# Second FFNs of a decoder trunk: three of four down pairs as seven half products

## The reference

```python
D_MODEL, SEQ, DEPTH, D_FF = 1024, 512, 2, 2816

def rms_norm(x, gain):
    xf = x * lax.rsqrt(jnp.mean(x * x, axis=-1, keepdims=True) + NORM_EPS)
    return xf * gain

def swiglu(x, w1, w3, w2):
    return (jax.nn.silu(x @ w1) * (x @ w3)) @ w2

for l in range(DEPTH):
    x = x + 0.5 * swiglu(rms_norm(x, ffn1_norm[l]), ffn1_w1[l], ffn1_w3[l], ffn1_w2[l])
    x = x + mixing(x)          # four branches, gates, W_out: not touched
    x = x + 0.5 * swiglu(rms_norm(x, ffn2_norm[l]), ffn2_w1[l], ffn2_w3[l], ffn2_w2[l])
```

## Time and profile before

| | us |
|---|---|
| median of 3 runs (lowest, highest) | 2750.36 (2749.57, 2750.45) |
| span of the profiled execution | 2748.1 |
| PE busy | 2743.3 |
| DVE busy | 1851.7 |
| ACT busy | 1335.1 |
| POOL busy | 940.7 |

### The profile page before, as it was taken

The page is one execution under the profiler, slowest core; times in us unless marked ns, Lnnn a source line. Parts: engine busy times, 40 slices in busy tenths (PEclk is TensorE's granted clock), DMA queues, the critical chain, the costliest instruction groups (busy, mean ns, idle before and its releaser), DMA issues.

```text
span 2748.1 us, 41845 instructions
## 1 busy us (share of the span) xinstructions
PE 2743.3 (100%) x16054; PEld 2337.2 (85%) x16054; DVE 1851.7 (67%) x2984; ACT 1335.1 (49%) x2103; POOL 940.7 (34%) x466
## 2 busy tenths in 40 slices
PE   9999999999999999999999999999999999999999
PEld 8898888777788889898998988887777888898988
DVE  7686857885667448585785878578846674585755
ACT  6353444655355346353563534446553653553533
POOL 0135824433343442131121357244333434421221
DMA  5333583222222232233332335832222222322332
GB/s 171 108 108 116 151 180 107 84 71 72 83 85 85 85 100 94 92 116 100 108 108 92 116 115 159 171 108 84 70 73 81 86 83 85 100 99 94 108 98 102
DMA packets 113110, 284.80 MB, mean 104 GB/s; under 512 B 35617, under 2 KB 45345, under 8 KB 112417
## 3 DMA queue, kind: packets, MB, share of 16 engines
q1 hardware_dynamic: 112928, 282.35, 34.6%
HBM read 268.67 MB, written 9.44 MB: 101 GB/s over the span
## 4 chain that ended last, share of the span: by engine, by line
PE 99%; DVE 1%; ACT 0%; issue 0%; DVEq 0%; ACTq 0%
PE bank L627 22%; PE bank L629 22%; PE bank L628 22%; PE bank L676 7%; PE bank L677 7%; PE bank L678 7%; PE bank L653 1%; PE bank L655 1%; PE bank L654 1%; PE bank L1048 1%; PE bank L1067 1%; PE bank L1082 1%; PE bank L817 1%; PE bank L1181 1%; PE bank L1035 0%; PE bank L1240 0%
## 5 line engine op out<-in xcount | busy, mean ns | idle before, releaser
L476 POOL TENSOR_TENSOR w_lo<-raw,w_hi 128x1024 fp32r<-128x1024 f32 x208 | 519.8, 2504 | 872.1 <-ACT w_hi L468 872.1
L627 PE MATMUL bank<-h_hi,w_hi 128*128 128x512 f32 x1504 | 593.4, 395 | 0.5 <-DVE silu_a L2363 0.3
L629 PE MATMUL bank<-h_hi,w_lo 128*128 128x512 f32 x1504 | 585.8, 390 | 0.0
L628 PE MATMUL bank<-h_lo,w_hi 128*128 128x512 f32 x1504 | 585.8, 390 | 0.0
L468 ACT ACTIVATE w_hi<-raw 128x1024 fp32r<-128x1024 f32 x310 | 326.5, 1056 | 353.8 <-PE bank L629 313.5
L541 POOL TENSOR_TENSOR w_lo<-raw,w_hi 128x1024 fp32r<-128x1024 f32 x122 | 223.4, 1854 | 802.3 <-DVE bank L2308 802.3
L627 PEld LDWEIGHTS bank<-h_hi,w_hi 128*128 128x128 f32 x1504 | 282.3, 188 | 65.6 <-issue 7.1
L629 PEld LDWEIGHTS bank<-h_hi,w_lo 128*128 128x128 f32 x1504 | 282.4, 188 | 59.8
L628 PEld LDWEIGHTS bank<-h_lo,w_hi 128*128 128x128 f32 x1504 | 282.5, 188 | 56.4
L627 PE MATMUL bank<-g_hi,w_hi 128*128 128x512 f32 x698 | 271.9, 390 | 0.0
L628 PE MATMUL bank<-g_lo,w_hi 128*128 128x512 f32 x698 | 271.7, 389 | 0.0
(11 more groups left out here) (452 smaller groups left out, 5895.7 us busy)
## 6 DMA issues: line engine op xcount, KB each, us to landing
raw<-in_w_lots SPq DMA_DIRECT2D x478, 512.0 KB, 3.7
s_wd<-s_z SPq DMA_DIRECT2D x8, 512.0 KB, 2.7
s_t<-s_taps SPq DMA_DIRECT2D x16, 256.0 KB, 12.9
...
```

The lines of the kernel that those rows point to most:

```text
L476: eng.tensor_tensor(w_lo[:, s], raw[:, s], w_hi[:, s].bitcast(f32), SUB).then_inc(S["lo_done"], 1)
L627: pe.matmul(b[:, :], w_hi[:, s, kw], xh[:, k], start=(k == 0), stop=False)
L628: pe.matmul(b[:, :], w_hi[:, s, kw], xl[:, k], start=False, stop=False)
L629: return pe.matmul(b[:, :], w_lo[:, s, kw], xh[:, k], start=False, stop=(k == nk - 1))
```

## The change

In both second FFNs the down stages of the first two thirds change, four stages in all (two layers, two thirds); "n" is the first lot of such a stage. The pair n, n+1 stays plain, but both lots run side by side over the tiles of g in the order 0, 4, 1, 5, 2, 6, 3, 7. The three pairs behind it (the first of them is called d) are done in seven half products, with the blocks of g_hi and g_lo where the up pairs have h, and with four sums of g. What goes with it:

- `gated` products of these thirds go to their own tile g_whole[:, i] (in the place of g_lo), and VectorE makes the sums of g tile by tile (`sums_of_g(k)` from tiles k and k+4: four instructions of 128x256, all operands in SBUF), the last two sets behind the last up pair.
- The low parts of g move from VectorE to GpSimd (`lows_of_g`), in the order in which the sums free them; behind them GpSimd also makes the w_lo of the three halved down pairs.
- ScalarE rounds the four sums (`round_gs`, 4 x 128x256 each). S3 and S4 are rounded into parts of g_lo and g_hi, so they wait for the plain pair. VectorE subtracts their low parts (`low_gs`, 4 x 128x256 each, SBUF).
- VectorE adds the results to x with `down_v`, `down_w`, `down_y`, `down_x` and `take_down_y`, of 128x256 each, and makes weight sums for three pairs more.
- Part of the sums lies over the constants hgreset, which layer 0 loads again (one DMA of 256 KB).

```diff
+DOWN_HALVED = ((), (0, 1))
+DOWN_ORDER = (0, 4, 1, 5, 2, 6, 3, 7)
+GS_ORDER = S1, S2, S3, S4
@@ memory
+        g_whole = at("g_whole", [P, 8, SEQ], f32, Y)
+        gs_hi = {S1: at("gs_hi1", [P, 4, HALF], f32r, A)[:, :, :], S2: at("gs_hi2", [P, 4, HALF], f32r, A + 2)[:, :, :],
+                 S3: g_lo[:, 0:4, HALF:SEQ], S4: g_hi[:, 0:4, HALF:SEQ]}
@@ TensorE; q1 to q7 take x = up_x or Down(which, th)
+                def ready(self, j):
+                    pe.wait_ge(S["c_ones_g_lo"], LOADED + gs_at(self.which, self.th, GS_ORDER.index(j)))
+            def down_halved(which, th, n, g0):
+
+                for j in range(2):
+                    begin(n + j, 0, OUT[n + j])
+                for i, k in enumerate(DOWN_ORDER):
+                    pe.wait_ge(S["g_done"], g0 - KT + i + 1)
+                    for j in range(2):
+                        m = passes(bank[OUT[n + j] % 4], slot(n + j), k, g_hi, g_lo, k, KT)
+                        if k == KT - 1:
+                            m.then_inc(S["out_done"], 1)
+                halved(n + 2, n + KT, Down(which, th))
...
-                    down(n, J, g0)
+                    down_halved(1, th, n, g0)
@@ SyncE
+                    if n == FIRST_LOT[1][2] + 8 and layer < DEPTH - 1:
+                        sp.wait_ge(S["out_done"], OUT[FIRST_LOT[1][2]])
+                        sp.dma_start(con[:, reset:reset + SEQ], con_in[:, reset:reset + SEQ]).then_inc(S["c_rest"], 16)
@@ GpSimd
+            def lows_of_pair(n):
+                pool.wait_ge(S["x7_in_t_sum"], t_at(n, T3))
+                low_of(pool, n)
+                low_of(pool, n + 1, 4)
+
+            def lows_of_g(which, th, g0):
+
+                for k in range(4):
+                    pool.wait_ge(S["x4_in_g_sum"], 2 * LOADED + gs_at(which, th, k))
+                    for i in (k, k + 4):
+                        pool.wait_ge(S["g_hi_done"], g0 + i + 1)
+                        pool.tensor_tensor(g_lo[:, i], g_whole[:, i], g_hi[:, i].bitcast(f32), SUB).then_inc(S["g_done"], 1)
...
+                    if th in DOWN_HALVED[which]:
+                        lows_of_g(which, th, g0)
+                        n = FIRST_LOT[which][th] + 2 * J
+                        pool.wait_ge(S["lo_done"], LOT(n + 2))
+                        for i in range(1, KT // 2):
+                            lows_of_pair(n + 2 * i)
@@ ScalarE
+            def round_gs(which, th, j, g0):
+                act.wait_ge(S["x4_in_g_sum"], 2 * LOADED + gs_at(which, th, 3))
+                if j in (S1, S2):
+                    act.wait_ge(S["gated_done"], g0)
+                else:
+                    act.wait_ge(S["out_done"], OUT[FIRST_LOT[which][th] + 2 * KT + 2])
+                for k in range(4):
+                    ins = act.activation(gs_hi[j][:, k], gs_sum[j][k], AFT.Copy)
+                ins.then_inc(S["x6_in_g_hi"], 1)
+
+            def down_halved(which, th, n, g0):
+
+                d = n + 2
+                round_gs(which, th, S1, g0)
+                round_t(d, T1)
+                round_t(d, T3)
+                round_gs(which, th, S2, g0)
+                high(act, d + 1, 4)
+                round_t(d, T2)
+                round_t(d, T4)
+                round_gs(which, th, S3, g0)
+                copy_x(d)
+                round_gs(which, th, S4, g0)
+                for a in range(d, n + KT, 2):
+                    high(act, a + 2)
+                    if a > d:
+                        copy_x(a)
+                    round_weights(a + 2, a)
@@ VectorE
+            def sums_of_g(which, th, k, g):
+
+                V.wait_ge(S["gated_done"], g + k + 4 + 1)
+                one, two = slice(0, HALF), slice(HALF, SEQ)
+                a11, a12, a21, a22 = g_whole[:, k, one], g_whole[:, k + 4, one], g_whole[:, k, two], g_whole[:, k + 4, two]
+                s1 = do(TT(gs_sum[S1][k], a21, a22, SUB))
+                do(TT(gs_sum[S3][k], a11, a21, SUB))
+                need(s1)
+                chain(TT(gs_sum[S2][k], gs_sum[S1][k], a11, SUB))
+                TT(gs_sum[S4][k], a12, gs_sum[S2][k], ADD).then_inc(S["x4_in_g_sum"], 1)
+
+            def low_gs(which, th, j):
+                V.wait_ge(S["x6_in_g_hi"], 2 * LOADED + gs_at(which, th, GS_ORDER.index(j)))
+                for k in range(4):
+                    ins = TT(gs_lo[j][k], gs_sum[j][k], gs_hi[j][:, k].bitcast(f32), SUB)
+                ins.then_inc(S["c_ones_g_lo"], 1)
+
+            def take_down_y(n, i):
+                take_y(n, 0)
+                done_v[0] = do(STT(x[:, i + 1, HALF:SEQ], v_sb[:, :], 0.5, x[:, i + 1, HALF:SEQ], MUL, ADD))
...
+            def down_halved(which, th, n):
+
+                d = n + 2
+                add_t(d, T1)
+                add_t(d, T3)
+                low_gs(which, th, S1)
+                low_t(d, T1)
+                add_t(d, T2)
+                low_t(d, T3)
+                low_gs(which, th, S2)
+                low_t(d, T2)
+                add_t(d, T4)
+                low_t(d, T4)
+                for j in range(2):
+                    down(n, j, 0)
+                low_gs(which, th, S3)
+                for a in range(d, n + KT, 2):
+                    i = a - n
+                    if a > d:
+                        down_v(a - 2, i - 2)
+                        down_w(a - 2, i - 2)
+                    add_t(a + 2, T1)
+                    add_t(a + 2, T3)
+                    low_t(a + 2, T1)
+                    if a > d:
+                        down_y(a - 2, i - 2)
+                    else:
+                        low_gs(which, th, S4)
+                        take_down_y(a, i)
...
@@ VectorE, halved: at the end of a pair's turn, and behind the last pair
+                    if whole and i - 2 >= KT // 2:
+                        sums_of_g(1, th, i - 2 - KT // 2, g0)
...
-                low_g(J - 2, g0)
+                if whole:
+                    sums_of_g(1, th, J - 2 - KT // 2, g0)
+                else:
+                    low_g(J - 2, g0)
                 take_first(a, J - 1)
                 take_x(a, J - 1)
                 need(done[(J - 1) % 2])
-                multiply(J - 1, g0)
+                multiply(J - 1, g0, whole)
+                if whole:
+                    sums_of_g(1, th, J - 1 - KT // 2, g0)
+                    return
```

More of the change, by code:

```diff
@@ L177 @@
                 HALVED_IN[_l][_n] = HALVED_IN[_l][_n + 1] = sum(len(_d) // 2 for _d in HALVED_IN)
+            for _i in range(1, KT // 2 if _th in DOWN_HALVED[_f] else 0):
+                _n = FIRST_LOT[_f][_th] + 2 * _j + 2 * _i
+                HALVED_IN[_l][_n] = HALVED_IN[_l][_n + 1] = sum(len(_d) // 2 for _d in HALVED_IN)
 LOT_AT = {MIX[_i]: MIX0 + _i for _i in range(MIX_LOTS)}
@@ new lines, in blocks_of, with __init__, ready @@
+            def blocks_of(whole, k0, cols):
+                return [whole[:, k0 + k, cols] for k in range(4)]
+            one, two = slice(0, HALF), slice(HALF, SEQ)
+            class Up:
+                x11, x12, x22 = ([blocks_of(a, k0, cols) for a in (h_hi, h_lo)] for k0, cols in ((0, one), (4, one), (4, two)))
+                sums = [[blocks_of(a[j], 0, one) for a in (s_hi, s_lo)] for j in range(4)]
+                def ready(self, j):
+                    pass
+            class Down:
+                x11, x12, x22 = ([blocks_of(a, k0, cols) for a in (g_hi, g_lo)] for k0, cols in ((0, one), (4, one), (4, two)))
+                sums = [[[gs_hi[j][:, k] for k in range(4)], gs_lo[j]] for j in S_SUMS]
+                def __init__(self, which, th):
+                    self.which, self.th = which, th
+                def ready(self, j):
+                    pe.wait_ge(S["c_ones_g_lo"], LOADED + gs_at(self.which, self.th, GS_ORDER.index(j)))
@@ L717, in q7, with halved @@
+            def q7(n, x):
                 pe.wait_ge(S["x5_in_yv"], y_at(n))
-                with_sums(x_bank(n), n, T3, S3).then_inc(S["x1_in_prod"], 1)
-            def halved(n, i0, J):
-                first = n + 2 * i0
-                for a in range(first, n + 2 * J, 2):
-                    q1(a)
+                x.ready(S3)
+                with_sums(x_bank(n), n, T3, x.sums[S3]).then_inc(S["x1_in_prod"], 1)
+            def halved(first, to, x):
+                for a in range(first, to, 2):
+                    q1(a, x)
@@ L2408, in three_plain @@
             def three_plain(n, g, which):
+                whole = 0 in DOWN_HALVED[which]
                 low_sum(2 * which)
```

204 lines of the change are left out of this document (123 added, 81 removed).

## The result

The changed kernel takes 2799.5 us (median of 5, 2799.3 to 2800.8), the kernel before 2749.8 us beside it: ratio 1.0182, 95% interval 1.017 to 1.0195. It is slower by 49.7 us, where 49.6 had been forecast.

A forecast was written before the change was run, and what follows sets the result against it. TensorE, busy 100% of the span, was taken as the bound. Walking through a site gave 14.9 us of waits less 2.5 gained, +12.4, or +49.6 for four sites: 2750.4+49.6 = 2800 us, range 2768 to 2818.

The forecast's parts named there:

- The gain: TensorE, halved down pairs: one eighth less arithmetic saves 0.84 us a pair, 2.5 us a site, 10.1 us in all.
- g_lo(3), g_lo(7): Plain down lots: TensorE waits for GpSimd's low parts of g tiles 3 and 7, 1.5 and 0.35 us a site.
- q1 for w_lo(d): First halved pair: TensorE's half product 1 waits 1.2 us a site for GpSimd's low part of d's weights.
- q5 for t_lo: First halved pair: TensorE's half product 5 waits 1.2 us a site for VectorE's low part of a weight sum.
- q6 for copy_x: First halved pair: half product 6 waits 4.5 us a site for ScalarE's copy, queued behind roundings.
- q7 for take_y: First halved pair: half product 7 waits 5.5 us a site for VectorE's take_y, queued behind low_gs(S4).
- next pair: Second halved pair: TensorE loses another 0.7 us a site before half product 7, its take_y being late again.
- Rival 3: TensorE's clock falls to 1.2 GHz in the new long waits, adding 2.3 to 4.5 us a site: 2812 us; chance 0.13.
- Rival 1: VectorE and GpSimd don't wait for one another in the down stages: +1.4 us a site, 2756 us; chance 0.08.
- Rival 2: Down stages: VectorE is in time for TensorE, so the whole gain arrives: 2740.3 us; chance 0.08.
- Rival 4: The change doesn't do what it says in matmuls per pair and GpSimd's g_lo; only a few per cent.
- The open bound: Down stages: add_t(T1) and add_t(T3), writing PSUM, taken to wait for GpSimd; if not, 0.8 us less a site.

The follow-up runs named there:

- both narrow: Changed kernel with GpSimd's low parts cut to 8 of 512 columns for g and 2 of 128 for halved down weights: 2753.7 us, ratio 1.0013.
- the run with fillers: Changed kernel plus 30 and 36 extra 256-column matmuls on TensorE before q6 and q7 of the first halved down pair: 2795.6 us, ratio 1.0166.

## Why the prediction was right, and where it was not

**The gain** of 2.5 us a site: with both narrow, the stage is 43.90 = 43.55 - 2.51 + 2.44 of wait + 0.4, so it holds.

**The waits,** per site, predicted against measured in the first one (excess of start over pitch):

| wait | predicted | measured |
|---|---|---|
| g_lo(3), g_lo(7) | 1.5, 0.35 | 1.0, 0.2 |
| q1 for w_lo(d) | 1.2 | 1.0 |
| q5 for t_lo | 1.2 | 1.2 |
| q6 for copy_x | 4.5 | 4.5 |
| q7 for take_y | 5.5 | 3.2 |
| next pair | 0.7 | 0 |
| slow clock and rest | 0 | 3.9 |
| sum | 14.9 | 15.0 |

**The mis-sized terms** are the last three: the walk left the clock at its full level. In truth it fell in the wait for q6, and the two products in front of q7 took 2.1 us more (4.96 for 2.87, from 1139.23 to 1144.19), out of a wait that VectorE ends at a time of its own: T+30.3 was measured for q7, T+30.8 walked. The 3.9 us of the row "slow clock and rest" are these 2.1, the 1.5 us that the clock costs from q7 on, and 0.3 of short waits. Rival 3 named this fall but put 2.3 to 4.5 us a site on top of the waits; the run with fillers puts it at 1.5 (6.0 us in all). Against it stand 0.7 walked for the next pair, which did not wait, and 0.9 by which the waits for g_lo and w_lo were walked too long. So the sum came out to 0.1 us, but that close only by luck: without the clock a site would have come out 1.4 us under the 14.9, 6 us in all. The chance of rival 3 (0.13) was too low for its mechanism and its price too high.

**Rival 1** is refuted by the means (1037 ns where 688 is the duration alone); its number for a kernel without turns came near, 2756 against 2753.7 measured with both narrow, though some 2.6 us of the difference to before are the clock's, which this rival did not have. **Rival 2,** the whole gain, was never reached, even by kernels rid of the lock or ordered from a trace. **Rival 4:** the counts of matmuls and of GpSimd's instructions are those of the order.

**The open bound:** add_t(T3), which writes PSUM, waits too (1.77 us at 1125.03 and once in each other site, mean of all 73 of its line 751 ns; 694 with both narrow), as was taken. The Trainium skill (SBUF — State Buffer, section SBUF: two separate sides) speaks of VectorE operations with two SBUF inputs; the trace agrees that the inputs decide.
